# Output projections of a state-space and a recurrent layer by seven products of halves instead of eight

## The reference

```
# first block, layer 0, mamba2_mixer
yg = (y.reshape(b, s, SSM_D_INNER) * silu(z)).reshape(b, s, G, SSM_D_INNER // G)
yg = yg * lax.rsqrt(mean(square(yg), axis=-1) + NORM_EPS)
yg = yg.reshape(b, s, SSM_D_INNER) * norm_w
mix = yg @ w_out                                  # 256x2048 @ 2048x1024
h = layer_norm(DEEPNORM_ALPHA * h + mix, ...)
h = layer_norm(DEEPNORM_ALPHA * h + hier_moe(h, ...), ...)
...
# second block, layer 1, odd_layer
y = lru_direction(forward) + lru_direction(reverse)
y = y * silu(gate)
h = h + einsum('bte,ed->btd', y, w_out)           # (256 + 16 meta)x2048 @ 2048x1024
return h[:, N_META:]
```

## Time and profile before

| | us |
|---|---|
| median of 3 runs | 1821.1 |
| lowest, highest | 1820.7, 1822.19 |
| the profiled execution | 1822.1 |
| its span, first to last instruction | 1820.3 |
| TensorE busy | 1798.2 |
| VectorE busy | 679.9 |
| ScalarE busy | 448.2 |

### The profile page before, as it was taken

One profiled execution on the slowest core, in us unless ns is written; L12 is line 12 of the kernel. 1 busy time (PEld: TensorE's weight loads), 2 busy tenths in 40 slices (PEclk: granted clock), 3 DMA queues, 4 the chain that ended last, 5 costly groups with the idle time before them and its releaser, 6 DMA issues.

```text
span 1820.3 us, 21314 instructions
## 1 busy us (share of the span) xinstructions
PE 1798.2 (99%) x8662; PEld 994.2 (55%) x8697; DVE 679.9 (37%) x1640; ACT 448.2 (25%) x958; POOL 69.8 (4%) x66
## 2 busy tenths in 40 slices
PE   9999999999999999999999999999999999999999
PEld 8888744443443433455444344343366767468875
DVE  3565434222212213036421221221345566235653
ACT  2332212111111100133211111110035534217752
POOL 0000000000000000000000000000011100001100
PEclk9999999999999999999999999999999999999999
DMA  9733459999999999808899999999932332140502
GB/s 378 310 127 139 162 207 387 421 428 427 428 427 428 427 428 426 323 0 341 359 417 429 427 427 427 428 426 427 424 149 82 143 136 93 41 168 24 231 1 116
DMA packets 44245, 527.42 MB, mean 290 GB/s; under 512 B 4784, under 2 KB 8528, under 8 KB 11120
## 3 DMA queue, kind: packets, MB, share of 16 engines
q1 hardware_dynamic: 41616, 516.70, 68.3%
q10 hardware_dynamic: 2528, 9.31, 1.3%
HBM read 524.91 MB, written 1.08 MB: 289 GB/s over the span
## 4 chain that ended last, share of the span: by engine, by line
PE 88%; DMA 9%; DVE 2%; ACT 0%; issue 0%; SPq 0%; POOL 0%; DVEq 0%; ACTq 0%
PE ps L211 38%; PE ps L811 20%; PE ps L846 10%; DMA ring<-in_wu 6%; PE ps L745 4%; PE ps L863 3%; DMA ring<-in_w_lat 2%; PE ps L1601 2%; PE ps L1169 1%; PE ps L643 1%; PE ps L818 1%; PE ps L1381 1%; PE ps L1394 1%; PE ps L740 0%; PE ps L1328 0%
## 5 line engine op out<-in xcount | busy, mean ns | idle before, releaser
L811 PE MATMUL ps<-ring,work 128*64 128x512 f32 x1856 | 409.1, 593 | 6.6 <-DMA ring<-in_wu 6.2
L211 PE MATMUL ps<-xl,ring 128*128 128x256 f32 (+3 forms) x1344 | 291.5, 375 | 0.8 <-DMA ring<-in_w_x 0.8
L811 PEld LDWEIGHTS ps<-ring,work 128*64 128x64 f32 x1856 | 131.5, 137 | 271.5 <-issue 250.2
L211 PEld LDWEIGHTS ps<-xl,ring 128*128 128x128 f32 x1344 | 243.7, 190 | 39.9 <-issue 2.5
L211 PE MATMUL ps<-ring,big 128*128 128x512 f32 (+1 forms) x480 | 197.5, 565 | 0.4 <-ACT big L1865 0.2
L846 PE MATMUL ps<-ring,work 128*64 128x512 f32 x816 | 181.5, 594 | 0.1
L211 PE MATMUL ps<-ring,xl 128*128 128x256 f32 (+1 forms) x576 | 176.0, 463 | 0.2 <-ACT xl L1686 0.2
L2469 DVE TENSOR_TENSOR work<-work,ps 128x512 f32<-128x512 f32 x32 | 22.0, 688 | 363.5 <-PE ps L811 343.9
L211 PEld LDWEIGHTS ps<-ring,xl 128*128 128x128 f32 x576 | 108.3, 190 | 59.3 <-issue 49.9
L211 PEld LDWEIGHTS ps<-ring,big 128*128 128x128 f32 x480 | 89.4, 190 | 93.2 <-issue 91.2
L846 PEld LDWEIGHTS ps<-ring,work 128*64 128x64 f32 x816 | 56.2, 137 | 100.3 <-issue 98.7
(11 more groups left out here) (439 smaller groups left out, 1769.7 us busy)
## 6 DMA issues: line engine op xcount, KB each, us to landing
ring<-in_wg SPq DMA_DIRECT2D x62, 2048.0 KB, 21.2
ring<-in_wu SPq DMA_DIRECT2D x52, 2048.0 KB, 22.3
ring<-in_wd SPq DMA_DIRECT2D x48, 2048.0 KB, 22.6
xl<-in_wd SPq DMA_DIRECT2D x10, 2048.0 KB, 24.2
xl<-in_wu SPq DMA_DIRECT2D x9, 2048.0 KB, 19.3
ring<-in_w_odd SPq DMA_DIRECT2D x8, 2048.0 KB, 7.5
ring<-in_w_xz SPq DMA_DIRECT2D x7, 2048.0 KB, 22.0
ring<-in_w_qkv SPq DMA_DIRECT2D x6, 2048.0 KB, 37.6
```

Source lines behind the costliest of these rows:

```text
L211: i = e.matmul(bout, lhs(k), rhs(k), start=start and k == ks[0], stop=stop and k == ks[-1])
L811: last = e.matmul(b[64 * j:64 * j + 64, :], x[:, 4 * a + k, 64 * j:64 * j + 64], w[k // 2][:, 2 * (k % 2) + j, :], start=a + k == 0, stop= ...
```

## The change

**Seven products.** Take the activations as A with halves A(t, i), t the token tile and i the parity of the row block, and the weights as B(i, n), n the output half. The four results C(t, n) = A(t, 0) B(0, n) + A(t, 1) B(1, n) are eight products. They are now seven (`p1` to `p7`), of sums that VectorE forms:

- weights: t1 = B01 - B00, t3 = B11 - B01 (in B01's slot), t2 = t3 + B00 (in B00's), t4 = B10 - t2 (in B10's)
- activations: s1 = A10 + A11, s3 = A00 - A10, s2 = s1 - A00, s4 = A01 - s2
- products: p1 = A00 B00, p2 = A01 B10, p3 = s4 B11, p4 = A11 t4, p5 = s1 t1, p6 = s2 t2, p7 = s3 t3

Products that share a result are added up in one PSUM bank (p1, p6 and p7 in one, p5 and p3 in another), and VectorE adds the bank's state to the rows of `h` in between. Only the row blocks that are there early take part: 14 of 16 in the state-space layer (7 matmuls a product instead of 8), 12 of 16 in the odd layer (6 matmuls a product). The remaining two or four blocks are multiplied as before: `tensor_last_group`, 8 matmuls, and `tensor_odd_late`, 4 blocks. The host now stores `ssm_out` and `odd_out` with even and odd row blocks apart (`in_turn`).

The diff, cut to what is spoken of:

```diff
-        for k0 in (0, 8):
-            for n in range(2):
-                ring.add(("wo", k0, n), 1, out_mm(k0, 1, n))
+        ring.add(("sum",), 0, out_mm("p5"))
+        WO = [(0, 0, "c21"), (1, 1, "p3"), (0, 1, "p7"), (1, 0, "p4")]
+        for hf, n, last in WO:
+            ring.add(("wo", hf, n), 1, out_mm(last))
...
+        def tensor_mix(e, name):
+            lhs, rhs = {
+                "p1": (ya(0, 0), wo(0, 0)), "p5": (ysum, kview(8, 512)(ring.view("sum"))), "p2": (ya(0, 1), wo(1, 0)),
+                "p6": (ya(0, 0), wo(0, 0)), "p3": (ya(0, 1), wo(1, 1)), "p7": (ya(1, 0), wo(0, 1)),
+                "p4": (ya(1, 1), wo(1, 0))}[name]
...
+            for m in range(7):
+                last = e.matmul(oacc[name][:, :], lhs[:, m, :], rhs[:, m, :], start=m == 0 and name in ("p1", "p5", "p2"),
+                                stop=m == 6, skip_group_check=True)
...
                     if g == 7:
-                        tensor_out(e, 0, part // 2, part % 2)
+                        tensor_mix(e, ("p1", "p5", "p2", "p6")[part])
...
-            for t in range(2):
-                for n in range(2):
-                    tensor_out(e, 8, t, n)
+            for name, t, n in (("c11", 0, 0), ("c22", 1, 1), ("c12", 0, 1), ("c21", 1, 0)):
+                tensor_last_group(e, name, t, n)
+            for name in ("p3", "p7", "p4"):
+                tensor_mix(e, name)
...
             for cb in range(8):
-                if cb == 7:
-                    tensor_odd_out(e, 0, 8, 0)
                 tensor_odd_gates(e, cb)
...
-            tensor_odd_out(e, 0, 8, 1)
-            for k0, k1 in ((8, 14), (14, 16)):
-                for n in range(2):
-                    tensor_odd_out(e, k0, k1, n)
+            for name in SEVEN:
+                tensor_odd_mix(e, name)
+            e.wait_ge(*y_in(6))
+            tensor_odd_late(e, (12, 13))
+            e.wait_ge(*y_in(7))
+            tensor_odd_late(e, (14, 15))
...
+                if g == 5:
+                    e.tensor_tensor(wsumv, wflat(0, 1), wflat(0, 0), ALU.subtract).then_inc(*mix.up("t1"))
+                elif g == 6:
+                    e.tensor_tensor(wflat(0, 1), wflat(1, 1), wflat(0, 1), ALU.subtract).then_inc(*mix.up("t3"))
+                elif g == 7:
+                    e.tensor_tensor(ysum, ya(1, 0), ya(1, 1), ALU.add).then_inc(*mix.up("s1"))
...
+            e.tensor_tensor(wflat(0, 0), wflat(0, 1), wflat(0, 0), ALU.add).then_inc(*mix.up("t2"))
...
+            e.tensor_tensor(wflat(1, 0), wflat(1, 0), wflat(0, 0), ALU.subtract).then_inc(*mix.up("t4"))
...
+                if cb == 5:
+                    e.tensor_tensor(wsum2[0], oflat(0, 1, 0, 2048), oflat(0, 0, 0, 2048), ALU.subtract
+                                    ).then_inc(*odd_mix.up("t1a"))
+                    e.tensor_tensor(wsum2[1], oflat(0, 1, 2048), oflat(0, 0, 2048), ALU.subtract).then_inc(*odd_mix.up("t1"))
+                elif cb == 6:
+                    e.tensor_tensor(oflat(0, 1), oflat(1, 1), oflat(0, 1), ALU.subtract).then_inc(*odd_mix.up("t3"))
...
-                e.dma_start(xT[:, 4 * j:4 * j + 4, 0:256],
-                            A["xT"][:, 1024 * j:1024 * j + 1024].rearrange("p (k t) -> p k t", k=4)).then_inc(x_in[j], 16)
-                e.dma_start(w0[:, :, 256 + 128 * j:384 + 128 * j], A["w_x0"][j].rearrange("p (k n) -> p k n", k=8)
-                            ).then_inc(first_in[j], 16)
+                half = slice(1024 * j, 1024 * j + 1024)
+                e.dma_start(xl[:, half], A["xT"][:, half]).then_inc(x_in[j], 16)
+                e.dma_start(ring.view("w", 0)[:, half], A["w_x0"][j]).then_inc(first_in[j], 16)
```

More of the change, by code:

```diff
@@ L244, in build @@
         y_norm, tr_y, ygT_in = sig("y_norm", G8), sig("tr_y", G8), sig("ygT_in", G8)
-        out_mm = sig("out_mm", (0, 8), range(2), range(2))
+        MIX = ("p1", "p5", "p2", "p6", "c11", "c22", "c12", "c21", "p3", "p7", "p4")
+        out_mm = sig("out_mm", MIX)
+        mix = sig("mix", ("t1", "t3", "s1", "s3", "r11", "s2", "t2", "r22", "s4", "t4", "r12", "c11", "d22", "c12", "r21",
+                          "c22", "c21"))
         L2, P16 = range(2), range(NE // 2)
@@ L325, in build @@
         OUT = ((0, 0, 0, 512), (0, 1, 0, 512), (1, 0, 0, 512), (1, 1, 0, 256), (1, 1, 256, 256))
-        oo_mm = Sig(mm_cb.sem, [(k, n, t, c) for k in (0, 8) for n, t, c, _ in OUT], mm_cb)
+        SEVEN = ("p1", "p5", "p2", "p6", "p3", "p7", "p4")
+        oo_mm = Sig(mm_cb.sem, [(x,) for x in SEVEN] + [x[0:3] for x in OUT], mm_cb)
+        odd_mix = then(mix, ("t1a", "t1", "t3", "s1", "s3", "r11", "s2", "t2", "r22", "s4", "t4", "r12", "r21", "r2b"))
         oc_in, sq_in, b_in, y_in = then(gained, G8, range(2)), then(xd_in, G8), then(dec_d, G8), then(dec_in, G8)
@@ L419, in build @@
                 ring.add(("ow", cb + 1), 1, og_mm(cb + 1, 1), E)
[L420 to L422 removed]
+        ring.add(("oo", 0, 0), 1, oo_mm(1, 1, 256), E)
+        ring.add(("oo", 0, 1), 1, oo_mm(1, 1, 256), E)
+        ring.last(ring.chunks["lru", 1][0])
+        ring.add(("oo", 1, 1), 1, oo_mm(1, 1, 256), E)
+        ring.add(("oo", 1, 0), 1, oo_mm(1, 1, 256), E)
         ygT = area(big, 0, (16, 256))
@@ new lines, in tensor_last_group @@
+        def tensor_last_group(e, name, t, n):
+            if name == "c11":
+                e.wait_ge(*ygT_in(7))
+            elif name == "c22":
+                e.wait_ge(*dec_d(7, 1))
+                e.wait_ge(*ring("wo", 1, 1))
+            elif name == "c12":
+                e.wait_ge(*mix("r22"))
+            else:
+                e.wait_ge(*mix("c11"))
+                e.wait_ge(*mix("t4"))
+            for hf in range(2):
+                last = e.matmul(oacc[name][:, :], ygT[:, 14 + hf, t * 128:(t + 1) * 128], wo(hf, n)[:, 7, :],
+                                start=hf == 0 and name in ("c22", "c21"), stop=hf == 1, skip_group_check=True)
+            last.then_inc(*out_mm.up(name))
@@ new lines, in tensor_odd_mix @@
+        def tensor_odd_mix(e, name):
+            lhs, rhs = {
+                "p1": (yo(0, 0), oo(0, 0)), "p5": (ysum2, None), "p2": (yo(0, 1), oo(1, 0)), "p6": (yo(0, 0), oo(0, 0)),
+                "p3": (yo(0, 1), oo(1, 1)), "p7": (yo(1, 0), oo(0, 1)), "p4": (yo(1, 1), oo(1, 0))}[name]
+            first = name in ("p1", "p5", "p2", "p4")
+            if first:
+                b, gone = eb.oldest(("oo", OB[name]))
+                if gone:
+                    e.wait_ge(*gone)
+            if name == "p1":
+                e.wait_ge(*ring("oo", 0, 0))
+                e.wait_ge(*y_in(5))
+            elif name == "p5":
+                e.wait_ge(*odd_mix("s1"))
+            elif name == "p2":
+                e.wait_ge(*ring("oo", 1, 0))
+            elif name == "p6":
+                e.wait_ge(*odd_mix("t2"))
+            elif name == "p3":
+                e.wait_ge(*odd_mix("s4"))
+            elif name == "p7":
+                e.wait_ge(*odd_mix("r12"))
+            elif name == "p4":
+                e.wait_ge(*odd_mix("t4"))
+            for k in range(6):
+                w = rhs[:, k, :] if rhs is not None else wsum2[k // 4][:, k % 4 * 512:k % 4 * 512 + 512]
+                last = e.matmul(eb["oo", OB[name]][:, :], lhs[:, k, :], w, start=first and k == 0, stop=k == 5,
+                                skip_group_check=True)
+            last.then_inc(*oo_mm.up(name))
@@ L1615, in tensor_odd_out, with tensor_odd_late @@
+        def tensor_odd_late(e, ks):
+            for n, t, c, w in OUT:
+                own = ("f" if n else "c") if t == 0 else ("e" if n == 0 else "a") if c == 0 else "g"
+                if own == "g" and ks[0] == 12:
+                    b, gone = eb.oldest(("oo", "g"))
                     if gone:
                         e.wait_ge(*gone)
-                last = project(e, eb["oo", n, t, c][:, 0:w], lambda k: yT[:, k, 16 + t * 128:144 + t * 128],
-                               lambda k: wv[:, k - c0, c:c + w], range(k0, k1), start=k0 == 0, stop=k1 == 16)
@@ L1619, in tensor_odd_out @@
-                if k0 != 8:
-                    last.then_inc(*oo_mm.up(c0, n, t, c))
+                if (n, t, c) == (1, 1, 0):
+                    e.wait_ge(*odd_mix("r2b"))
+                for k in ks:
+                    last = e.matmul(eb["oo", own][:, 0:w], yT[:, k, 16 + t * 128:144 + t * 128], oo(k % 2, n)[:, k // 2, c:c + w],
+                                    start=own == "g" and k == 12, stop=k == ks[-1], skip_group_check=True)
+                if ks[-1] == 15:
+                    last.then_inc(*oo_mm.up(n, t, c))
```

202 lines of the change are left out of this document (152 added, 50 removed).

## The result

| | before | after |
|---|---|---|
| median, us | 1821.01 (4 runs) | 1808.38 (4 runs) |
| lowest, highest | 1820.7, 1822.19 | 1808.06, 1809.13 |
| the profiled execution, its span | 1822.1, 1820.3 | 1808.5, 1806.7 |

The ratio of the runs is 0.9928, 95% interval 0.9915 to 0.994, some 13 us; the medians lie 12.6 us apart, the two traces 13.6. The forecast was 1809.1 us, 12.0 us faster.

The account below looks back on a forecast made before the run. TensorE's instructions were taken to bound the kernel; 6.0 (state-space layer) + 5.2 (odd layer) + 0.77 (first loads) = 12.0 us gave a forecast of 1809.1 us, range 1807.9 to 1813.0.

Parts of the forecast that it names:

- the odd layer's term of 5.2 us: Odd output projection: 58 calls for 64, six at 0.858 us, 5.15 us, with fewer half-width calls 5.2 us.
- The bound: Whole kernel: TensorE busy 1798.2 of 1820.3 us, so the span is the sum of its instructions.
- Seven calls in the state-space layer, 6.0 us: State-space output projection: 57 calls instead of 64, seven saved at 0.858 us each, 6.0 us.
- 48 calls' worth: Odd projection before the change: 41.79 us read as 48 calls, the 256-wide ones counted half.
- The first loads, 0.77 us: Kernel start: 4 KB pieces land before the warm-up ends, removing TensorE's 0.77 us wait for the first weights.
- nothing moves before 2 us: Kernel start: no data moves before 2 us; support for the rival that first loads bring nothing, chance 0.12.
- The wide sums: VectorE's weight additions: 3.84 us for 128x3584, 3.31 for 3072, 2.27 and 1.21 for 2048 and 1024.
- The covers: VectorE's sums finish before TensorE needs them: 1.4 us to spare in group 7, 1.0 at p3, the thinnest.
- the rival of a thin cover: VectorE's wide sums or waits run longer, so TensorE waits at p3 and group 7: 1810.5 to 1812 us; chance 0.14.
- The expert stream: Expert weight loads: the queue's idle time takes their delay, so the state-space layer's 6.0 us come through.
- point from which it decides: Slower rival, chance 0.03: later expert loads decide once the queue's idle 15 us shrink below some 4.
- The waits on `wu`: Expert layers: TensorE's waits for the expert weights stay near 8.6 us in sum.

Follow-up runs that it names:

- late_p3: The changed kernel with the first output-projection weight slot of the state-space layer released by p3 instead of c21; 1816.4 us (8 runs).
- cover_1: The changed kernel with one useless 128x1024 VectorE operation at each of the two thinnest covers; 1808.66 us (4 runs).
- cover_3: The changed kernel with one useless 128x3072 VectorE operation at each of the two thinnest covers; 1814.33 us (5 runs).

## Where the prediction held, and which step failed

The mechanism held: the gain is TensorE's removed calls, nothing waited for VectorE's sums, and the expert stream did not swallow it. The size was too small, 12.0 us for 12.6 between the medians. The step that failed is the odd layer's term of 5.2 us, 0.35 too small. The rest of the difference is less than two executions differ by.

- **The bound.** Right: TensorE's instructions are the span, and each call removed counted.
- **Seven calls in the state-space layer, 6.0 us.** Measured 6.00 us, and the same in every undisturbed trace. The 18.19 us row is 21 calls of 0.858 and a drain of 0.17 (what the last row of a block takes beyond the distance from row to row).
- **Six calls in the odd layer, 5.2 us: the step that failed.** Measured 5.55. I had read the 41.79 us as "48 calls' worth", so as matmuls alone. But 48 x 0.858 is 41.18 us, 41.35 with a drain; 0.44 us were left over, and I put them at nothing. 0.35 of them are TensorE's wait for `y_in(6)`, which the new order removes as well, since the scan of block 6 now ends long before the late blocks are multiplied; I had named no wait of TensorE there. The half-width calls were priced nearly right: 0.432 us against half of 0.858, so 0.06 us for the 24 fewer, where the forecast put 0.05.
- **The first loads, 0.77 us.** 0.8 us on average over the traces, 0.43 in the one shown. The size was right, the reason not quite: I had taken the end of the warm-up, 6.79 us, as fixed. Its 28 rows took 5.73 to 6.27 us in the four traces with the old loads and 4.77 to 5.86 in the nine with the new ones and 28 rows, so it ended at 5.8 us in after; the first product then starts at 6.4, where the weights land, or at the warm-up's end where that is later (6.74 in late_p3). On average it came 1.1 us earlier. Why the warm-up's length varies stays open. That the later pieces come earlier with the first was true of most traces: `z0dt` landed at 20.9 to 21.2 us in the four with the old loads and at 19.1 to 20.0 in seven of the nine with the new ones in their place, but at 20.90 and 21.24 in the two of after, where TensorE waited for it. The Trainium skill (DMA: Bandwidth & Descriptors, Specifications) asks for at least 512 B for the full rate, by which this term would have been 0; the traces don't agree. The first half of `w_x0` landed at 7.30 to 7.86 us in pieces of 512 B and at 6.30 to 6.47 in pieces of 4 KB. The first half of `xT`, in pieces of 1 KB before, landed at 5.0 to 5.4 us in both. Whether the pieces' size or the strides do it was not taken apart. That "nothing moves before 2 us" was not so: before moved 20 GB/s from 1 to 2 us, after 33.
- **The wide sums.** 3.84, 3.31, 2.27 and 1.21 us forecast; 3.88, 3.35, 2.28 and 1.22 measured. The Trainium skill (VectorE: DVE Perf Modes, The TRN2 errata) gives a formula with a fixed 151 cycles beside one an element. An estimate by it is 3.89 us for 3584 and 3.36 us for 3072; the trace agrees.
- **The covers.** In group 7 1.4 us forecast, 1.45 measured (228.51 to 229.96); at p3 1.0 forecast, 1.2 measured (s4 ends at 1773.47; p3 follows 24 rows behind 1764.41, at 1774.7). Between the decay products and L2394 stand five operations, not six. cover_1 and cover_3 show that the covers are real and that past them each us is paid. By them the rival of a thin cover would have happened with sums 1.2 us longer.
- **The expert stream.** "The 6.0 us come through" was right, the working was loose. I had the loads through at 270.7 and 274.4 us. The half of `wg` that TensorE wants second is issued at 267.8 only, behind a wait of its own, and landed at 277.2. Its cover shrank from 4.8 to 1.4 us, and I had neither priced it nor named it as thin. The "point from which it decides" was looked for in the queue's idle time; it is this one load's cover.
- **The rest.** 1.6 us of the difference between the two traces came from the two expert layers, where no term stood. Some 1.0 of it is the spread of executions; whether the other 0.66 is the slots' stays open. The waits on `wu`, forecast to stay near 8.6 us, were 6.7 in after and 7.4 in its second trace.

## To carry to other kernels

Removed calls can be summed from one row of the trace when the engine has no idle time. But multiply the price out over the whole block first: what the block takes beyond it can be a wait too short to show, and it may go with the calls or stay. When a change makes loads later and their users earlier, follow each load to the instruction that wants it: the sum of a queue's idle time says nothing of the last load in it. And before a us is explained, take a second trace of the same kernel: here the expert layers, which wait for DMA, moved by up to 1.3 us between two traces of one kernel, and the start by 0.3; the stages without such waits moved by less than 0.1.
